# Spreading routing weights with one 256-wide product per token, and moving a weight split from VectorE to GpSimd

## The reference, cut to what matters

```
i1, i2  = indices of the two half keys (0..127 each)      expert = i1 * 128 + i2
g       = softmax(top, axis=-1)                            # 128 gates per token
act     = gelu(einsum('td,ted->te', xb, u[eid]))
out     = einsum('te,ted->td', g * act, v[eid])
```

## Time and profile before

| | |
|---|---|
| median of 3 runs | 3087.43 us (3076.34 to 3116.95) |
| profiled execution, own time | 3071.83 us |
| its span, first to last instruction | 3070.0 us |
| mean granted PE clock | 0.953 |
| PE, DVE, ACT, POOL busy | 93%, 65%, 48%, 11% |

### The profile page before, as it was taken

The page is one execution under the profiler, slowest core; times in us unless marked ns, Lnnn a source line. Parts: engine busy times, 40 slices in busy tenths (PEclk is TensorE's granted clock), DMA queues, the critical chain, the costliest instruction groups (busy, mean ns, idle before and its releaser), DMA issues.

```text
span 3070.0 us, 57118 instructions
## 1 busy us (share of the span) xinstructions
PE 2845.2 (93%) x19490; PEld 2645.5 (86%) x19490; DVE 1999.1 (65%) x4265; ACT 1466.4 (48%) x2409; POOL 338.6 (11%) x167
## 2 busy tenths in 40 slices
PE   7889889999999998868899999999997989999998
PEld 6878788999988887858899999988886879997998
DVE  5545962877467766685598788467766675555655
ACT  4444344444455555454444444455554454444443
POOL 0002685000000000000079000000000000000000
PEclk8999999999999998889999999999998999995999
DMA  3434456545676664314355554676665314560454
GB/s 149 165 137 151 148 195 206 177 171 179 226 253 239 239 240 158 125 68 151 119 182 204 185 173 173 217 251 239 239 240 208 138 69 167 191 225 9 157 187 165
DMA packets 140448, 546.15 MB, mean 178 GB/s; under 512 B 15784, under 2 KB 81592, under 8 KB 83616
## 3 DMA queue, kind: packets, MB, share of 16 engines
q1 hardware_dynamic: 63216, 455.38, 41.3%
q10 hardware_dynamic: 73728, 67.14, 6.9%
q0 software_dynamic: 3376, 21.88, 1.9%
HBM read 505.53 MB, written 40.91 MB: 178 GB/s over the span
## 4 chain that ended last, share of the span: by engine, by line
PE 74%; DVE 9%; DMA 6%; ACT 4%; POOL 4%; issue 3%; SPq 0%; ACTq 0%; DVEq 0%
PE bank L709 21%; PE bank L710 21%; PE bank L711 21%; POOL wL L503 4%; PE bank L884 4%; DMA ring<-in_w_stream 3%; ACT wH L493 3%; DMA act_parked<-act_out 2%; DVE wL L503 2%; PE bank L785 1%; PE bank L803 1%; PE bank L794 1%; DVE act_out L1558 1%; PE bank L722 1%; DVE h L1582 1%
## 5 line engine op out<-in xcount | busy, mean ns | idle before, releaser
L503 DVE TENSOR_TENSOR wL<-ring,wH 128x1024 fp32r<-128x1024 f32 x744 | 909.5, 1225 | 760.1 <-ACT wH L493 759.5
L709 PE MATMUL bank<-hnH,wH 128*128 128x256 f32 x3648 | 1061.5, 291 | 61.6 <-DVE hnL L1540 31.0
L493 ACT ACTIVATE wH<-ring 128x1024 fp32r<-128x1024 f32 x864 | 909.2, 1055 | 341.5 <-DMA ring<-in_w_stream 163.9
L710 PE MATMUL bank<-hnL,wH 128*128 128x256 f32 x3648 | 1043.9, 286 | 0.0
L711 PE MATMUL bank<-hnH,wL 128*128 128x256 f32 x3648 | 1043.4, 286 | 0.0
L709 PEld LDWEIGHTS bank<-hnH,wH 128*128 128x128 f32 x3648 | 710.6, 195 | 73.4 <-issue 43.4
L710 PEld LDWEIGHTS bank<-hnL,wH 128*128 128x128 f32 x3648 | 711.3, 195 | 0.1
L711 PEld LDWEIGHTS bank<-hnH,wL 128*128 128x128 f32 x3648 | 709.9, 195 | 0.0
L709 PE MATMUL bank<-wH,wgtH 128*128 128x512 f32 x1024 | 399.1, 390 | 4.9 <-issue 4.5
L711 PE MATMUL bank<-wH,wgtL 128*128 128x512 f32 x1024 | 398.7, 389 | 0.0
L710 PE MATMUL bank<-wL,wgtH 128*128 128x512 f32 x1024 | 398.7, 389 | 0.0
(11 more groups left out here) (345 smaller groups left out, 3447.3 us busy)
## 6 DMA issues: line engine op xcount, KB each, us to landing
ring<-in_w_stream SPq DMA_DIRECT2D x432, 1024.0 KB, 4.9
act_parked<-act_out ACTq DMA_DIRECT2D x256, 128.0 KB, 3.6
act_in<-act_parked ACTq DMA_DIRECT2D x256, 128.0 KB, 2.7
sw_bias<-in_c_swa POOLq DMA_DIRECT2D x1, 4096.0 KB, 15.4
relb_rows<-rel_table POOLq DMA_DIRECT2D x1, 2048.0 KB, 9.4
h_parked<-h POOLq DMA_DIRECT2D x2, 1024.0 KB, 6.5
h_back<-h_parked POOLq DMA_DIRECT2D x2, 1024.0 KB, 6.6
od_relb<-relb_rows POOLq DMA_DIRECT2D x2, 1024.0 KB, 7.5
```

The source lines that it names most:

```text
L493: eng.activation(wH[:, b % NBUF, :], raw(b), ACT.Copy).then_inc(w_high, 1)
L503: eng.tensor_tensor(wL[:, b % NBUF, :], raw(b), wH[:, b % NBUF, :].bitcast(F32), ALU.subtract).then_inc(w_low, 1)
L709: pe.matmul(dst, lh, rh, start=start, stop=False, skip_group_check=True)
L710: pe.matmul(dst, lh, rl, start=False, stop=False, skip_group_check=True)
```

## The change

The one-hot tile of the first index becomes 256 wide: the left half carries the high part of the gate, the right half the low part. One DVE instruction (`scalar_tensor_tensor`) writes both halves. The operands are fp32r now, so that PE makes one 256-wide fp32r product per token in place of one 128-wide float32 product. Two tokens fill a bank, and tokens go in pairs, one pair in the middle of an act block and one behind it. ACT copies the high half of the bank into `gates`, and DVE adds the low half from the bank. The high and low parts of all gates are made once per layer, ahead of the stage. The low parts of the weight blocks of the token stage are made by POOL in place of DVE (POOLED goes from 43 to 107).

```diff
-POOLED = AHEAD + 3
+POOLED = AHEAD + T // 4 + 3
+PAIRS = T // 2
...
-        (onehot,) = stage(("onehot", [16, P], F32))
+        second, first_by_gate, gate_hl = stage(("second", [4, P], F32R), ("first_by_gate", [4, 2, P], F32R),
+                                               ("gate_hl", [2, T], F32R))
...
                 def tokens(i, j):
-                    if not isinstance(i, int):
-                        pe.wait_ge(g_read, i * 4 + (l * T // 4 + j + 1 - BANKS))
+                    if not isinstance(i, int) or j >= BANKS:
+                        pe.wait_ge(g_read, i * 8 + (l * PAIRS + j + 1 - BANKS))
                     elif j >= NT:
                         evacuated(BANKS + j)
-                    pe.wait_ge(onehots, i * 4 + (l * T // 4 + j + 1))
-                    for m in range(4):
-                        k = (4 * j + m) % 8
-                        last = pe.matmul(psacc[j][:, m * P:(m + 1) * P], onehot[:, k, :], onehot[:, 8 + k, :],
-                                         start=True, stop=True)
+                    pe.wait_ge(onehots, i * 8 + (l * PAIRS + j + 1))
+                    for m in range(2):
+                        k = (2 * j + m) % 4
+                        last = pe.matmul(psacc[j % BANKS][:, m * 2 * P:(m + 1) * 2 * P], second[:, k, :],
+                                         first_by_gate[:, k].rearrange("p a b -> p (a b)"), start=True, stop=True)
                     last.then_inc(g_done, 1)
...
                 with pe.Fori(1, T // 16) as i:
                     for j in range(4):
-                        acts(i, AHEAD + j)
-                        tokens(i, j)
+                        acts(i, AHEAD + j, (i, 2 * j))
+                        tokens(i, 2 * j + 1)
...
                 def gated(i, j):
-                    act.wait_ge(g_done, i * 4 + (l * T // 4 + j + 1))
-                    act.activation(gates[:, :, bass.ds(i * 16 + 4 * j, 4)],
-                                   psacc[j][:, :].rearrange("p (t n) -> p n t", t=4), ACT.Copy).then_inc(g_read, 1)
+                    pair = psacc[j % BANKS][:, :].rearrange("p (t h n) -> p t h n", t=2, h=2)
+                    act.wait_ge(g_done, i * 8 + (l * PAIRS + j + 1))
+                    act.activation(gates[:, :, bass.ds(i * 16 + 2 * j, 2)].rearrange("p n t -> p t n"),
+                                   pair[:, :, 0, :], ACT.Copy).then_inc(g_half, 1)
...
                 with act.Fori(0, T // 16) as i:
                     for j in range(4):
+                        gated(i, 2 * j)
                         acted(i, AHEAD + j)
-                        gated(i, j)
+                        gated(i, 2 * j + 1)
...
                 def rows(i, j):
-                    if not isinstance(i, int) or j >= 2:
-                        dve.wait_ge(g_done, i * 4 + (l * T // 4 + j - 1))
-                    for m in range(4):
-                        k = (4 * j + m) % 8
-                        tok = i * 16 + (4 * j + m)
-                        dve.tensor_scalar(onehot[:, k, :], iota, slotT[:, 2, bass.ds(tok, 1)], None, ALU.is_equal)
-                        last = dve.tensor_scalar(onehot[:, 8 + k, :], iota, slotT[:, 1, bass.ds(tok, 1)],
-                                                 slotT[:, 0, bass.ds(tok, 1)], ALU.is_equal, ALU.mult)
+                    for m in range(2):
+                        k = (2 * j + m) % 4
+                        tok = i * 16 + (2 * j + m)
+                        dve.tensor_scalar(second[:, k, :], iota, slotT[:, 2, bass.ds(tok, 1)], None, ALU.is_equal)
+                        last = dve.scalar_tensor_tensor(
+                            first_by_gate[:, k], spread(iota, 1, 2), slotT[:, 1, bass.ds(tok, 1)],
+                            gate_hl[:, :, bass.ds(tok, 1)].bitcast(F32).broadcast_to([P, 2, P]), ALU.is_equal, ALU.mult)
                     last.then_inc(onehots, 1)
+                def gated(i, j):
+                    pair = psacc[j % BANKS][:, :].rearrange("p (t h n) -> p t h n", t=2, h=2)
+                    two = gates[:, :, bass.ds(i * 16 + 2 * j, 2)].rearrange("p n t -> p t n")
+                    dve.wait_ge(g_half, i * 8 + (l * PAIRS + j + 1))
+                    dve.tensor_tensor(two, pair[:, :, 1, :], two, ALU.add).then_inc(g_read, 1)
...
                 with dve.Fori(1, T // 16) as i:
-                    for j in range(4):
+                    for j in range(8):
+                        dve.wait_ge(g_done, i * 8 + (l * PAIRS + j - 1))
                         rows(i, j)
-                        split_low(dve, b0 + POOLED + j, i)
+                        gated(i, j - 2)
```

More of the change, by code:

```diff
@@ L462, in build_stacks @@
         cq_sq_s, mla_n, mla_qk, ff_low = sem("cq_sq"), sem("mla_normed"), sem("mla_qk"), sem("ff_low")
+        gate_high, g_half = sem("gate_high"), sem("g_half")
         eps_set, sink_set = sem("eps_set"), sem("sink_set")
@@ L862, in evacuated, with acts @@
                     pe.wait_ge(read_by[reader[held[b]]], rank[held[b]])
-                def acts(i, c):
+                def acts(i, c, between=None):
                     if isinstance(i, int) and 4 * i + c < BANKS:
@@ L873, in acts @@
                                        both(hn, FULL, k), k == 0, k == DC - 1)
+                        if between and k == DC // 2 - 1:
+                            tokens(*between)
                     last.then_inc(u_done, 1)
                 def tokens(i, j):
-                    if not isinstance(i, int):
-                        pe.wait_ge(g_read, i * 4 + (l * T // 4 + j + 1 - BANKS))
+                    if not isinstance(i, int) or j >= BANKS:
+                        pe.wait_ge(g_read, i * 8 + (l * PAIRS + j + 1 - BANKS))
                     elif j >= NT:
                         evacuated(BANKS + j)
-                    pe.wait_ge(onehots, i * 4 + (l * T // 4 + j + 1))
-                    for m in range(4):
-                        k = (4 * j + m) % 8
-                        last = pe.matmul(psacc[j][:, m * P:(m + 1) * P], onehot[:, k, :], onehot[:, 8 + k, :],
-                                         start=True, stop=True)
+                    pe.wait_ge(onehots, i * 8 + (l * PAIRS + j + 1))
[3 more added lines that the diff above has]
+                                         first_by_gate[:, k].rearrange("p a b -> p (a b)"), start=True, stop=True)
                     last.then_inc(g_done, 1)
@@ L912, in peer @@
                 for j in range(4):
-                    acts(0, AHEAD + j)
-                    tokens(0, j)
+                    acts(0, AHEAD + j, (0, 2 * j))
+                    tokens(0, 2 * j + 1)
                 with pe.Fori(1, T // 16) as i:
                     for j in range(4):
-                        acts(i, AHEAD + j)
-                        tokens(i, j)
+                        acts(i, AHEAD + j, (i, 2 * j))
+                        tokens(i, 2 * j + 1)
                 with pe.Fori(0, (N_KEYS - AHEAD - T // 4) // 4) as i:
@@ L921, in peer @@
                         acts(i, AHEAD + T // 4 + j)
-                pe.wait_ge(g_read, (l + 1) * T // 4)
+                pe.wait_ge(g_read, (l + 1) * PAIRS)
                 for j in range(4):
@@ L1328, in peer @@
                     ps = take((p + "slotT", tt))
+                    act.activation(gate_hl[:, 0, tt * P:(tt + 1) * P], ps[:, 0:P], ACT.Copy).then_inc(gate_high, 1)
                     act.activation(slotT[:, :, tt * P:(tt + 1) * P], ps[:, 0:3 * P].rearrange("p (a b) -> p a b", a=3),
@@ L1700, in peer @@
                 b0 = BNO[(p + "u", 0)]
+                for tt in range(NT):
+                    dve.wait_ge(gate_high, NT * l + tt + 1)
+                link(dve.tensor_tensor(gate_hl[:, 1, :], slotT[:, 0, :], gate_hl[:, 0, :].bitcast(F32), ALU.subtract))
                 def rows(i, j):
-                    if not isinstance(i, int) or j >= 2:
-                        dve.wait_ge(g_done, i * 4 + (l * T // 4 + j - 1))
-                    for m in range(4):
-                        k = (4 * j + m) % 8
-                        tok = i * 16 + (4 * j + m)
-                        dve.tensor_scalar(onehot[:, k, :], iota, slotT[:, 2, bass.ds(tok, 1)], None, ALU.is_equal)
-                        last = dve.tensor_scalar(onehot[:, 8 + k, :], iota, slotT[:, 1, bass.ds(tok, 1)],
-                                                 slotT[:, 0, bass.ds(tok, 1)], ALU.is_equal, ALU.mult)
-                    last.then_inc(onehots, 1)
+                    for m in range(2):
[5 more added lines that the diff above has]
+                            gate_hl[:, :, bass.ds(tok, 1)].bitcast(F32).broadcast_to([P, 2, P]), ALU.is_equal, ALU.mult)
+                    last.then_inc(onehots, 1)
+                def gated(i, j):
[3 more added lines that the diff above has]
+                    dve.tensor_tensor(two, pair[:, :, 1, :], two, ALU.add).then_inc(g_read, 1)
                 def weigh(i, c):
@@ L1724, in weights_low @@
```

(20 more changed lines are left out.)

## The result

| | before | after | forecast |
|---|---|---|---|
| median | 3098.18 us (4 runs, 3076.34 to 3116.95) | 3299.81 us (4 runs, 3289.03 to 3324.94) | 3270 us, 3185 to 3350 |
| profiled execution | 3071.83 us | 3294.24 us | |
| mean granted PE clock | 0.953 | 0.940 | |

The ratio is 1.0665, with a 95% interval from 1.0564 to 1.0766. The kernel became slower by about 202 us by the medians, 222 us by the two profiled executions; the forecast was +198 us against the profiled one.

The account below looks back on a forecast made before the run. PE bound the token stage at 3.77 us a block; DVE, held by POOL, would become the bound at 5.3 us. 3071.8 + 196 + 2 for the gate parts gave 3270 us, range 3185 to 3350 us.

Parts of the forecast that it names:

- PE, 3.4 us a block, -47 us if it stayed the bound: Token stage: 28 products of 0.118 us plus two change-overs make 3.4 us a block against 3.77, saving 47 us.
- DVE's own work, 3.06 us: Token stage: one-hot instructions and adds take 1.53 us a pair, 3.06 us a block, with the add at 0.34.
- rival D: Single numbers 1 KB apart slow adds and copies: 5.84 us a block, +265 us, 3337 us; chance 0.10.
- The hold, 2.38 - 0.13 = 2.25 us: DVE stands still during POOL's 2.38 us split each block, less 0.13 us falling beside an add.
- Who is held: Both one-hot DVE instructions are held by POOL, with maxima near 2.4 to 2.8 us, one such per block.
- The add reads a bank and is not held: DVE's add of the low half reads a bank, so POOL's split does not hold it; no long maxima.
- The period, 5.3 us: Token-stage block: 3.06 + 2.38 - 0.13 = 5.3 us with DVE the bound, against 3.77: +196 us.
- rivals A and B: A: POOL and DVE do not meet, 3025 us, chance 0.15. B: only scalar_tensor_tensor held, 3200 us, chance 0.10.
- rival C: PE's clock falls to 0.50 in the token stage: 6.8 us a block, +388 us, 3460 us; chance 0.05.
- No idle DVE, no late split: Token stage: buffers and waits never let DVE idle, and POOL's late split delays nobody by itself.
- The base: Forecast built on the profiled 3071.8 us; the median before, 15.6 us higher, was left to the range.

Follow-up runs that it names:

- tiny_t_inner: Changed kernel with GpSimd's token-stage splits cut to 8 columns and gates touched in runs of two numbers: 3064.8 us, 0.9880 of the kernel before.
- iota_bank_t_inner: Changed kernel with the one-hot index row in a PSUM bank, two token banks and gates in runs of two numbers: 3043.3 us, 0.9857 of the kernel before.
- t_inner: Changed kernel with a pair's two tokens innermost in copy and add, so gates is touched in runs of two numbers: 3273.9 us, 1.0561 of the kernel before.
- before_pool: Kernel before with only the token-stage weight splits moved to GpSimd, float32 products and one-hot tiles kept: 3129.3 us, 1.0110 of the kernel before.
- iota_bank: Changed kernel with the one-hot index row copied once per layer into a PSUM bank, tokens sharing two banks: 3127.1 us, 1.0087 of the kernel before.
- pool_tiny: Changed kernel with each GpSimd token-stage split covering 8 of 1024 columns, so it computes something else: 3105.9 us, 1.0011 of the kernel before.

## Why the prediction was right, by its steps

- **PE, 3.4 us a block, -47 us if it stayed the bound.** Right: 3.39 us (tiny_t_inner, iota_bank_t_inner).
- **DVE's own work, 3.06 us.** The two one-hot instructions were right (276 and 473 ns by their medians). The add was mis-sized: 0.63 us from start to start in place of 0.34, which is 0.58 us a block. The forecast named the cause, took nothing for it and kept 0.54 as a bound (rival D). It took L1300 as the nearest row, which writes runs of 16 bytes and so could not show it. The rule that the prediction cites from the Trainium skill ("SBUF — State Buffer", Door 1: The DMA port swizzle) was the better guide. By the forecast's own list an add above 0.6 us speaks for D, and it came: D's term was real, 0.58 us, and D's sum of 5.84 us a block was still not reached, because the hold was shorter.
- **The hold, 2.38 - 0.13 = 2.25 us.** Right in kind, too large in size for the changed kernel. L1719 was busy 361.1 us for 512 x 0.276 = 141, and L1720 244.5 for 512 x 0.473 = 242: 222 us / 128 = 1.74 us a block. The forecast let the splits fall at random places and counted 0.13 us beside an add; it was 0.48 us, since the add was longer and most splits started in it or just before. Some 0.2 us more lay beside the instruction in flight, which the forecast left out. With the short add (t_inner) the same sum gives 2.05 us, in before_pool 2.18.
- **Who is held.** The forecast expected long maxima in both one-hot instructions. 125 of 512 tensor_scalars took over 1 us and only one scalar_tensor_tensor did; that either can be held is shown by t_inner. The splits had a median of 2.41 us, the longest 2.94 for 2.8 at most expected. PE's idle time in front of L889 was 1.5 us a block (193 / 128) for 1.9.
- **The add reads a bank and is not held.** Right, by the 45 adds above. The row that the forecast took it from shows little: L1546 starts 0.44 us before the end of the split, not in its middle.
- **The period, 5.3 us.** The sum as it should have been is 3.64 + 1.74 = 5.38; measured were 5.40 and 5.47. Two terms were wrong by +0.58 and -0.51 and nearly cancelled; that the total came so near was luck. Without it the forecast would still have held: t_inner is the kernel with the add that the forecast assumed, and it has 5.16 us a block, about 173 us over the kernel before.
- **One-hot tensor_scalar held or not (rivals A and B).** Held (before_pool). The step from 353 ns for 256 elements and 0.28 us for 128 to two elements a cycle, and from there to a hold, held good. It fits that the same instruction takes 62 ns more when it reads a bank (iota_bank_t_inner): that is the 63 ns between 70 and 133 ns for 128 elements, the prices of the two rates in the forecast.
- **PE's clock (rival C).** The granted clock was 0.94 in the stage, with PE busy 74%. It did not bind: DVE was busy 99.7%.
- **No idle DVE, no late split.** Right. POOL's split delayed nobody by its own lateness; no wait of PE for wL stands in the stage.
- **The base.** The forecast stayed at the profiled 3071.8 us, while the median of the runs before came out at 3098. That accounts for most of the 30 us by which the median after (3299.8) lies above 3270; the difference itself was forecast as 198 and measured as 202 us.

## What to carry to other kernels

Work moved from VectorE to GpSimd is only moved if the two do not meet: read one timeline where both are busy, and compare the maximum of each VectorE instruction with its median. Here a split cost VectorE 1.14 us when it made it and 1.7 to 2.2 us when GpSimd did; no hold was left once the one-hot instructions took their table from a PSUM bank, at a price of 62 ns for each tensor_scalar. When two tokens are written into a layout with a stride, put the small contiguous dimension innermost: the add took 421 ns in runs of 8 bytes, as long as an add of contiguous numbers (0.42 us), while runs of 4 bytes took 1.7 times as long in the add and 1.6 times in the copy.

## What the runs showed that was not expected

- A long-strided write hurts ACT as well: 640 ns against 405 for the same 256 numbers. When ACT's copy and DVE's add run together for over 0.2 us both get longer still, in the changed kernel to medians of 861 and 843 ns and to 912 and 902 ns at most.
- In iota_bank, the durations of DVE's instructions drift upward in layer two, while the distance from the start of one add to the next stays near 2.0 us:

```profile
L1723 DVE TENSOR_SCALAR second<-bank,slotT x512: 329/343/1401, 529.0 to 1979.7; 128x128 fp32r<-128x128 f32 x171
L1734 DVE TENSOR_TENSOR gates<-bank,gates x256: 700/858/1795, 532.9 to 1984.2; 128x256 f32 x120, 128x256 f32<-128x256 f32 x8
...
1853.42 1.25 DVE L1723 TENSOR_SCALAR second<-bank,slotT 128x128 fp32r<-128x128 f32 x1
1853.69 1.38 DVE L1724 SCALAR_TENSOR_TENSOR first_by_gate<-bank,slotT,gate_hl 128x256 fp32r<-128x256 f32 x1
1854.08 1.25 DVE L1723 TENSOR_SCALAR second<-bank,slotT 128x128 fp32r<-128x128 f32 x1
1854.34 1.39 DVE L1724 SCALAR_TENSOR_TENSOR first_by_gate<-bank,slotT,gate_hl 128x256 fp32r<-128x256 f32 x1
```

  These are not holds: each instruction still starts 0.26 to 0.39 us behind the one before it, and all of them are longer by some 0.9 us. It does not happen with runs of two. But the stride alone is not enough either: layer one of the same kernel has adds of 0.88 us at most, and pool_tiny, with the same strided writes, of 0.93. How it comes about stays open.
- POOL does not wait for VectorE to fall idle. With back-to-back one-hot instructions it got its turn behind the one in flight (602.67 in before_pool, where L1709 had started at 602.44), and in the stage of the changed kernel the median split took 2.41 us, hardly more than the 2.38 us of a split with nothing in its way.
